# The second feed-forward product of a decoder layer as seven half-size block products instead of eight

## The reference

```
h += sqrelu(RMSNorm(h) @ W1) @ W2          # W1 1024 x 4096, W2 4096 x 1024
h += sigmoid(RMSNorm(h) @ W_gate) * (p @ W_ple)
return rmsnorm(h, final_norm_g)
```

## Time and profile before

| | us |
|---|---|
| median of 3 runs (lowest, highest) | 771.75 (771.71, 771.85) |
| the profiled execution, its own time | 771.78 |
| its span, first to last instruction | 770.1 |
| TensorE busy | 757.4 |
| DVE busy | 436.1 |
| ACT busy | 326.3 |
| POOL busy | 87.4 |

### The profile page before, as it was taken

How to read it: one execution, slowest core, us unless ns; L and a number is a source line. 1 busy time by engine, 2 the same in 40 slices (tenths; PEclk the granted TensorE clock), 3 DMA queues, 4 the chain that set the end, 5 groups by cost and what they waited for, 6 DMA issues and landing times.

```text
span 770.1 us, 9090 instructions
## 1 busy us (share of the span) xinstructions
PE 757.4 (98%) x3492; PEld 623.7 (81%) x3492; DVE 436.1 (57%) x488; ACT 326.3 (42%) x456; POOL 87.4 (11%) x60
## 2 busy tenths in 40 slices
PE   8999999999999999999999999999999999999996
PEld 7888877887887888888888888888888888888885
DVE  5556894668569575547454443444444444446754
ACT  6525447645475812326443140413223140323556
POOL 1022210864562000000000000000000000000000
PEclk9999999999999999999999999999999999999999
DMA  9622323432422443123423232332323232332102
GB/s 334 191 83 83 109 79 119 133 109 87 161 82 83 144 157 136 42 69 108 127 93 110 82 110 96 95 107 84 109 82 109 82 100 96 102 120 82 47 0 110
DMA packets 35193, 81.88 MB, mean 106 GB/s; under 512 B 3924, under 2 KB 5592, under 8 KB 35160
## 3 DMA queue, kind: packets, MB, share of 16 engines
q1 hardware_dynamic: 33928, 77.20, 30.8%
q10 hardware_dynamic: 1232, 4.23, 1.7%
HBM read 79.28 MB, written 2.13 MB: 106 GB/s over the span
## 4 chain that ended last, share of the span: by engine, by line
PE 93%; DVE 3%; ACT 1%; issue 1%; DMA 1%; SPq 0%; ACTq 0%; DVEq 0%
PE acc L1122 29%; PE acc L1124 29%; PE acc L1123 29%; PE side L1184 3%; PE side L1277 2%; DVE w_lo L751 1%; PE side L1244 1%; DVE conv L948 1%; DMA gain<-in_norm_mix_g 1%; PE side L1284 1%; PE side L1272 1%; DVE h L937 0%; PE acc L1201 0%; ACT w_hi L431 0%; PE side L1224 0%
## 5 line engine op out<-in xcount | busy, mean ns | idle before, releaser
L1122 PE MATMUL acc<-w_hi,a_hi 128*128 128x512 f32 x512 | 204.2, 399 | 0.0
L1124 PE MATMUL acc<-w_hi,a_lo 128*128 128x512 f32 x512 | 199.7, 390 | 0.0
L1123 PE MATMUL acc<-w_lo,a_hi 128*128 128x512 f32 x512 | 199.3, 389 | 0.0
L431 ACT ACTIVATE w_hi<-w_raw 128x1024 fp32r<-128x1024 f32 (+1 forms) x128 | 130.2, 1036 | 145.5 <-PE acc L1124 143.3
L751 DVE TENSOR_TENSOR w_lo<-w_raw,w_hi 128x1024 fp32r<-128x1024 f32 (+1 forms) x128 | 166.1, 1298 | 45.0 <-ACT w_hi L431 44.3
L802 DVE TENSOR_TENSOR h<-h,acc 128x1024 f32<-128x1024 f32 x48 | 58.6, 1220 | 106.1 <-PE acc L1124 106.0
L1122 PEld LDWEIGHTS acc<-w_hi,a_hi 128*128 128x128 f32 x512 | 96.2, 188 | 21.0 <-issue 1.4
L1123 PEld LDWEIGHTS acc<-w_lo,a_hi 128*128 128x128 f32 x512 | 96.2, 188 | 20.7 <-issue 1.4
L1124 PEld LDWEIGHTS acc<-w_hi,a_lo 128*128 128x128 f32 x512 | 96.1, 188 | 20.4
L1122 PE MATMUL acc<-b_hi,w_hi 128*128 128x512 f32 x256 | 99.6, 389 | 0.0
L1123 PE MATMUL acc<-b_lo,w_hi 128*128 128x512 f32 x256 | 99.6, 389 | 0.0
(11 more groups left out here) (183 smaller groups left out, 818.7 us busy)
## 6 DMA issues: line engine op xcount, KB each, us to landing
w_raw<-in_w_ff SPq DMA_DIRECT2D x64, 512.0 KB, 3.5
w_raw<-in_w_in SPq DMA_DIRECT2D x36, 512.0 KB, 3.8
w_raw<-in_w_out SPq DMA_DIRECT2D x16, 512.0 KB, 3.4
h<-in_x SPq DMA_DIRECT2D x8, 512.0 KB, 4.3
seg<-cs_dram ACTq DMA_DIRECT2D x8, 512.0 KB, 3.8
w_raw<-in_w_ple_gate SPq DMA_DIRECT2D x8, 512.0 KB, 3.8
out<-y SPq DMA_DIRECT2D x4, 512.0 KB, 2.6
w_raw<-in_w_ple_proj SPq DMA_DIRECT2D x4, 256.0 KB, 2.6
```

Of the source, the lines that this page charges most:

```text
L431: act.activation(w_hi[:, half, 2 * p:2 * p + n, :], w_raw[:, p, 0:n, :], ACT.Copy).then_inc(hi_ready, 1)
L1122: pe.matmul(dst, st[0], mv[0], start=start, stop=False)
L1123: pe.matmul(dst, st[0], mv[1], start=False, stop=False)
L1124: return pe.matmul(dst, st[1], mv[0], start=False, stop=stop)
```

## The change

The hidden units are taken in four units of 1024 instead of eight pairs of 512. For each unit the second product is [A11 A12; A21 A22] times [B11 B12; B21 B22]: A is the unit's squares, positions halved (256) and hidden units halved (512); B is 1024 x 1024 of W2 in four quarters of 512 x 512. It is made in Winograd's form of seven products of 256 x 512 x 512 instead of eight, each of 24 matmuls:

- The sums of the activations S3 = A21 - A11, S1 = A21 - A22, S2 = A11 - S1, S4 = A12 - S2 are made by DVE; each, and A11 and both halves of A2, is split by ACT and DVE.
- The sums of the weights T3 = B12 + B22, T2 = B11 + T3, T1 = B12 + B11, T4 = T2 + B21 are made by transfers that GpSimd issues with an add (`t_add`), in two halves of 512 KB each, into the buffer of one operand. T1 needs B12 again, which SP reloads when T2 has landed (`reload_b12`).
- The order is B11, T3, T2, T1, T4, B21, B22. B11 and T1 accumulate in two banks of `side` each over all four units, the others go to `acc` and are added to quarters of `h` by DVE in each unit (`h_add`, six additions of 128 x 1024). `h` holds combinations of its quarters until six more operations of the last unit (`h_finish`), two of which read no PSUM.

The first product of a unit is made of four forms of 512 x 512 (two column blocks, each in two halves of k), 48 matmuls each. Forms stand in a ring of three (`ring`, hi beside raw, lo in the place of raw), 11 per unit; a form may be loaded, or a quarter's hi written, only when the product of the form three before has ended. DVE no longer squares; ACT does (`square`). All loops are written out. The stage's buffers lie where `w_raw`, `w_hi`, `w_lo`, `a_hi`, `a_lo` and `y` were; so the first W1 forms are loaded only when the output projection has ended (before, the first block was split beside the per-layer product), and the per-layer product is stored to DRAM and loaded again ahead of the gate. The first group of the stage uses bank 2 of `acc`, not bank 0. The norm ahead of the gate takes row tiles 2, 3, 0, 1 (`TILES`): 2 and 3 are final after T4, 0 and 1 after B22; the first tile is transposed in the middle of B22, the second in the middle of the first gate group, the others after the second. The gate takes both column halves of tiles 2 and 3 first, and its first group waits for the B22 addition.

The diff, cut (of the last lists DVE's order is the first, TensorE's the last):

```diff
+TILES = (2, 3, 0, 1)
...
+PRODUCTS = ("B11", "T3", "T2", "T1", "T4", "B21", "B22")
+A_FORMS = ("A11", "S3", "S2", "S1", "A22", "A12", "S4")
+QUARTER = {"T3": 0, "T1": 0, "B12": 0, "B11": 1, "T2": 1, "T4": 1, "B21": 2, "B22": 3}
...
+            def load_f1(n):
+                u, e = divmod(n, FORMS)
+                b, kh = 2 * u + e // 2, e % 2
+                if n >= 3:
+                    sp.wait_ge(ff_step, form_end(n - 3))
+                else:
+                    sp.wait_ge(acc_full, 4 * (OUT + 4) if n < 2 else 4 * (PLE + 1))
...
+            load_f1(2)
+            load_quarter(0, "B22")
+            load_quarter(0, "B21")
+            load_f1(3)
+            reload_b12(0)
+            for u in range(1, UNITS):
+                load_quarter(u, "B12")
+                load_quarter(u, "B11")
+                load_quarter(u, "B21")
+                load_f1(FORMS * u)
+                load_quarter(u, "B22")
+                for e in range(1, 4):
+                    load_f1(FORMS * u + e)
+                reload_b12(u)
...
+            def t_add(u, name, p):
+                at = (slice(None), slice(2 * p, 2 * p + 2))
+                k = 8 * u + 2 * p
+                if name == "T3":
+                    pool.wait_ge(q_landed[0][p], 16 * (2 * u + 1))
+                    pool.wait_ge(q_landed[3][p], 16 * (u + 1))
+                    src = quarter[3][at]
+                elif name == "T2":
+                    sum_landed(pool, u, "T3", p)
+                    pool.wait_ge(form_lo, form_count(u, "B11", p))
+                    src = quarter[0][at]
+                elif name == "T1":
+                    pool.wait_ge(q_landed[0][p], 16 * (2 * u + 2))
+                    src = w_ff2[:, k:k + 2, 0:512]
+                else:
+                    pool.wait_ge(form_lo, form_count(u, "T2", p))
+                    pool.wait_ge(q_landed[2][p], 16 * (u + 1))
+                    src = quarter[2][at]
+                pool.dma_start(quarter[QUARTER[name]][at], src, accum_op=ALU.add
+                               ).then_inc(t_landed[QUARTER[name]][p], 16)
...
+                if j < 4:
+                    act.wait_ge(f1_landed[n % 3][p], 16 * f1_use(n))
+                    src = raw[at]
+                else:
+                    name = PRODUCTS[j - 4]
+                    src = quarter[QUARTER[name]][at]
+                    if name in SUMS:
+                        sum_landed(act, u, name, p)
+                    else:
+                        act.wait_ge(q_landed[QUARTER[name]][p], 16 * (u + 1))
+                    act.wait_ge(ff_step, form_end(n - 3))
+                act.activation(hi[at], src, ACT.Copy).then_inc(form_hi, 1)
...
+                bank, hq, op = {
+                    "T3 right": (acc[:, 0:2, :], h22, ALU.add), "T3 above": (acc[:, 0:2, :], h12, ALU.subtract),
+                    "T2": (acc[:, 2:4, :], h22, ALU.add), "T4": (acc[:, 0:2, :], h21, ALU.add),
+                    "B21": (acc[:, 2:4, :], h11, ALU.add), "B22": (acc[:, 0:2, :], h12, ALU.add)}[what]
...
+                src, hq, op = {
+                    "B11 above": (side[:, 0:2, :], h11, ALU.add), "B11 right": (side[:, 0:2, :], h22, ALU.subtract),
+                    "T1 right": (side[:, 2:4, :], h22, ALU.add), "T1 left": (side[:, 2:4, :], h21, ALU.add),
+                    "C21": (h22, h21, ALU.subtract), "C12": (h22, h12, ALU.add)}[what]
...
+            for u in range(UNITS):
+                n = FORMS * u
+                if u:
+                    for p in range(2):
+                        split_form(n + 1, p)
+                    h_add(u - 1, "B22")
...
+                for p in range(2):
+                    split_form(n + 6, p)
+                split_a(u, "S2")
+                split_a(u, "S1")
+                split_a(u, "A2a")
+                split_a(u, "A2b")
+                for p in range(2):
+                    split_form(n + 7, p)
+                h_add(u, "T3 right")
+                h_add(u, "T3 above")
+                split_a(u, "S4")
+                if u == UNITS - 1:
+                    h_finish("B11 above")
+                    h_finish("B11 right")
+                for p in range(2):
+                    split_form(n + 8, p)
+                h_add(u, "T2")
+                for p in range(2):
+                    split_form(n + 9, p)
+                if u == UNITS - 1:
+                    h_finish("T1 right")
+                    h_finish("T1 left")
+                    h_finish("C21")
+                for p in range(2):
+                    split_form(n + 10, p)
...
+                    h_finish("C12")
+                h_add(u, "T4")
+                if u < UNITS - 1:
+                    h_add(u, "B21")
+                    for p in range(2):
+                        split_form(n + FORMS, p)
+            for p in range(2):
+                split_lo(GATE, p)
+            normed(2, 0)
+            normed(2, 1)
+            for p in range(2, 4):
...
+                    left, c0 = s_form[int(name[1])][0::2], 0
+                else:
+                    left, c0 = a2[0::2], 256 if name == "A22" else 0
+                bank = {"B11": side[:, 0:2], "T1": side[:, 2:4], "T3": acc[:, 0:2], "T2": acc[:, 2:4],
...
+                if i >= 4:
+                    pe.wait_ge(gate_act, i - 3)
+                else:
+                    pe.wait_ge(h_added, add_count(UNITS - 1, "B22" if i < 2 else "B21"))
...
+            gate(0, lambda: turn_norm(2, 1))
+            gate(1)
+            turn_norm(2, 2)
```

More of the change, by code:

```diff
@@ L177, in build_layer @@
         kind = {}
-        for b in range(GATE + 2):
+        for b in range(PLE + 1):
             if b in (OUT, OUT + 1, OUT + 2, OUT + 3):
@@ L259, in freed, with form_end, f1_use, product_end @@
             ins.then_inc(side_free[fills[name][0]], 1)
+        def form_end(n):
+            u, j = divmod(n, FORMS)
+            return STEPS * u + (4 * j + 4 if j < 4 else 16 + 2 * (j - 4) + 2)
+        def f1_use(n):
+            return sum(m % 3 == n % 3 and m % FORMS < 4 for m in range(n + 1))
+        def product_end(u, name):
+            return STEPS * u + 16 + 2 * PRODUCTS.index(name) + 2
+        def form_count(u, name, p):
+            return 2 * (FORMS * u + 4 + PRODUCTS.index(name)) + p + 1
+        def sum_landed(eng, u, name, p):
+            eng.wait_ge(t_landed[QUARTER[name]][p], 16 * (2 * u + (1 if name in ("T3", "T2") else 2)))
+        ADDS = ("T3 right", "T3 above", "T2", "T4", "B21", "B22")
+        LAST_ADDS = ("B11 above", "B11 right", "T1 right", "T1 left", "C21", "C12")
+        def add_count(u, what):
+            return 2 + len(ADDS) * u + ADDS.index(what) + 1
+        LO_COUNT = {"A11": 1, "S3": 2, "S2": 3, "S1": 4, "A22": 6, "A12": 6, "S4": 7}
         block = ctx.enter_context(nc.Block())
@@ new lines, in relu, with square @@
+            def relu(u, i):
+                n = 8 * u + i
+                act.wait_ge(ff_step, STEPS * u + (5 + i if i < 4 else 9 + i))
+                if n >= 2:
+                    act.wait_ge(hid_raw, n - 1)
+                else:
+                    wait_filled(act, ("xt", 1, 2 + i, 1))
+                act.activation(tmp[:, i % 2, :], acc[:, (i + 2) % 4, :], ACT.Relu).then_inc(relu_done, 1)
+            def square(u, i):
+                n = 8 * u + i
+                act.wait_ge(relu_done, n + 1)
+                if i == 0 and u:
+                    act.wait_ge(s_raw, 7 * u)
+                if i == 4 and u:
+                    act.wait_ge(ff_step, product_end(u - 1, "B21"))
+                dst = a1[:, i, :] if i < 4 else a2[1][:, i - 4, :]
+                act.activation(dst, tmp[:, i % 2, :], ACT.Square).then_inc(hid_raw, 1)
@@ L760, in normed @@
                 slot, use = ((0, 1), (0, 3), (1, 3))[n]
+                c = s if n < 2 else TILES[s]
                 if s == 0:
```

580 lines of the change are left out of this document (394 added, 186 removed).

## The result

The changed kernel takes 758.38 us (median of four runs, 758.33 to 760.71) against 771.75: a ratio of 0.9827, 95% interval 0.9815 to 0.984. The prediction was 757.4 us, faster. The profiled execution took 760.71 us (span 759.0, mean granted clock 0.991); the other three had a span of 756.6 us at 0.995.

What follows compares the result with a forecast made beforehand. TensorE, busy 757.4 of 770.1 us, was taken as the bound, so fewer matmuls pay in full. 771.8 - 21.8 + 1.2 (turns) + 1.1 (stage start) + 5.1 (stage end) = 757.4 us; range 754 to 770.

Steps and rivals of the forecast that it cites:

- The 96 matmuls, -21.8 us: Feed-forward second product: 672 matmuls instead of 768, each 0.2267 us, all of it on the path.
- No stall inside the second half of a unit: From B11 on in each unit, DVE's queue has each form 3 to 6 us ahead of its product.
- Rival (d): DVE takes 1.22 instead of 1.14 us each; last B22 late, turns lose cover: 762; 0.19 together with the clock rival.
- The adding transfers: Weight sums, eight of 512 KB per unit: occupancy 3.2 us, landing 5.1 us after 1 us on GpSimd, no stall.
- that sign: Sign of being right: T4's half sums land by 13 us after B11 in the units.
- The limit: Chain T2, reload of B12, T1, T4: 2L + 3s under 29.4, so occupancy s up to 5.1 us with L = s + 1.9.
- the rival: Slow sums make T4 and T1 late in each unit; gain spent at s = 5.8, 782 to 788 at 6.3; chance 0.13.
- Rival (b), sums held by DVE: GpSimd writes descriptors only while DVE pauses; T4 sums 7 us late per unit, 28 in all, 785; chance 0.06.
- The turns of the units, +1.2 us: Next unit's third group waits for B22's addition: 1.3 us of cover, 0.4 us lost at each of three turns.
- The start of the stage, +1.1 us: First group goes to bank 2, so TensorE waits for ACT's copy of the last per-layer product.
- The end of the stage, +5.1 us: Last unit, waits on DVE's queue: 0.2 us before B22, 1.0 in its middle, 3.9 before the first gate product.
- The clock, rival (c), 2.6 us: Wait before the gate drops the clock to 1.2 GHz, some 3 us more: 760.5; 0.19 together with slower DVE.

Runs made afterwards that it cites:

- e1: Changed kernel with the 24 matmuls of T3 done twice in each unit, so 96 matmuls are back: 780.36 us.
- e3: Changed kernel with one plain 512 KB copy issued by GpSimd ahead of each of the 32 adding transfers: 763.79 us.
- e4: Changed kernel with two plain 512 KB copies issued by GpSimd ahead of each of the 32 adding transfers: 808.5 us.
- e9: Changed kernel run again without an edit, beside the kernel before on one chip: ratio 0.9824; profiled execution 756.83 us.
- e6: Changed kernel with unit 0's first product beginning in bank 0 instead of bank 2: 758.69 us.
- e11: Changed kernel with e6's bank order, e7's edits, T4's addition ahead of C12, and B22's addition ahead of the next second form's splits at turns: 752.11 us.
- e7: Changed kernel with gate products beginning in banks 2 and 3, and DVE doing B21's addition and first tile's lo parts before two gate-weight splits: 755.30 us.
- e12: e11 with the first normalised tile ahead of the two splits of gate weights on DVE: 752.67 us.

## Why the prediction was right, step by step

**The 96 matmuls, -21.8 us.** Right: 21.6 in e1, 3396 instructions, and units 81.6 to 81.7 us apart.

**No stall inside the second half of a unit.** Right, and the ledger of DVE's queue holds. In unit 0 B11 starts at 413.9 us; the form T4 was put at 18.4 us behind it, and DVE ends it 18.9 behind, as the timeline of the kernel after shows. Rival (d), DVE at 1.22 instead of 1.14 us each, did not come: behind the split at 429.32 the next starts 1.13 us later. Only the two additions to h take 1.23 us each (two from 426.86 to 429.32).
```profile
426.86 2.54 DVE L1331 TENSOR_TENSOR h<-h,acc 128x1024 f32<-128x1024 f32 x2
429.32 1.22 DVE L1314 TENSOR_TENSOR s_lo<-s_raw,s_hi 128x1024 fp32r<-128x1024 f32 x1
430.45 2.35 DVE L1275 TENSOR_TENSOR ring_lo<-quarter,ring_hi 128x1024 fp32r<-128x1024 f32 x2
```

**The adding transfers.** Occupancy was taken as 3.2 us and measured at 2.9. The Trainium skill, "Collectives: The Full Stack", section on the bandwidth ceiling, has an adding transfer at half the rate of a copy; here it is 2.9 to 1.57, a factor of 1.86. Landing was put at 5.1 us after 1 us on GpSimd; the page has 6.1 from the issue. For T4 the landing was forecast by 13 us behind B11, and ACT took the second half up at 14.0, released by the transfer: 1 us later than that sign allowed, with 7 us of cover left to the 21 at which the prediction has it needed. The limit was mis-sized: it set L = s + 1.9, as for a transfer that has the engines for itself. In e3 the adding transfers landed after 10.5 us at s = 4.4, with a copy and loads on the same engines. The give-back starts below s = 4.4 and not at 5.1, and by the line it is half again as steep (30 and not 20 us for each us); the fallen clock of e4 is in that. By the estimate above the gain is spent at 4.7, not at the 5.8 of the prediction: the rival was nearer than told, though with the measured 2.9 us still well clear.

**Rival (b), sums held by DVE.** Empty. GpSimd's two issues of T4's sums in unit 0, and ACT's use of the second, in the timelines of the kernel after:
```profile
419.30 0.88 POOL L570 DMA_DIRECT2D quarter<-quarter  x1 [5.80 <-DVE ring_lo L1275]
420.43 0.85 POOL L570 DMA_DIRECT2D quarter<-quarter  x1 [0.25 <-DVE ring_lo L1275]
...
427.90 1.06 ACT L659 ACTIVATE ring_hi<-quarter 128x1024 fp32r<-128x1024 f32 x1 [1.75 <-DMA quarter<-quarter]
```
DVE is busy without a pause from 417.8 to 436 us, and the second sum has landed 7.5 us after its issue. The Trainium skill, "SBUF — State Buffer", section "Who interferes with whom", says that a sum of two tensors on DVE does not stall such a transfer; the trace agrees.

**The turns of the units, +1.2 us.** The cover was computed as 1.3 us; slower loads and sharing were then taken to use it up and 0.4 us more, a loss of 1.7. In the kernel after, B22's addition ends at 457.03 and the third group wants it at 457.47:
```profile
453.41 2.48 DVE L1275 TENSOR_TENSOR ring_lo<-ring_raw,ring_hi 128x1024 fp32r<-128x1024 f32 x2 [3.12 <-ACT ring_hi L659]
455.81 1.22 DVE L1331 TENSOR_TENSOR h<-h,acc 128x1024 f32<-128x1024 f32 x1
```
0.44 us of cover are left: the loss of cover was 0.9 and not 1.7, so there was no wait. In e9, the same kernel, the addition ends 2.0 us ahead at this turn, and in e6 and e3 there were waits of 0.36 and 0.42 us: the cover changes with the execution. The term should have been 0 to 0.4, not 1.2. With the order of e11, addition first, it ends 5.4 us ahead (451.92 for 457.30).

**The start of the stage, +1.1 us.** Right: 1.31 by the profile, 1.5 from start to start, with the releaser as named, and gone in e6.

**The end of the stage, +5.1 us.** Right in kind. By the profile's waits it is 4.4 us: 0.49, 0.62 and 3.28 us for 0.2, 1.0 and 3.9. The prediction reckoned from start to start; so counted it is 4.9 (0.65, 0.8 and 3.4), 0.2 less than forecast. The order of what waits for what was as computed. DVE's queue is unbroken from 671.5 to 702.7 us in the kernel after.

**The clock, rival (c), 2.6 us.** It was given as a case of its own with 3 us. It came in the profiled execution and, in six others with the same wait, in one more; the median does not hold it (758.38 against 760.71). It fits a term with a chance, not a case.

**What was missing.** The start of the kernel, early or late by 1.4 us, was not in the range of causes: the profile of before was of an early one. From start to start, the turns (-1.2), the end (-0.2) and the start of the stage (+0.4) came out 1.0 us better than forecast; the slower instructions behind the waits, some 0.5 us, had no term, and the late start cost 1.4: 757.4 - 1.0 + 0.5 + 1.4 = 758.3 against 758.38. The mechanism was right; that the number came within 1.0 us is in part luck, as a term of 1.2 us for waits that did not come made up for most of a loss that nobody had seen. Without the late start the kernel took 756.83.

## What to carry to other kernels

Where TensorE has no gap, matmuls taken out pay in full. What has to be worked out is the queue of the helpers in the shortest stretch, and the places where a stage begins and ends. Here the banks decided: let the first product of the next stage take the bank that comes free first (e6, and e7 with its order on DVE: 4.4 us here). Reordering a queue that has no pause moved the wait (e11, e12). Less work in it, or moving what is not needed ahead of the wait behind it, should shorten it; e7 did the second, together with its change of banks, and taking work out was not tried. A transfer that lay well hidden cost nothing until its cover ended, and then stalls, and with two copies the clock too: test the distance by slowing it, not by making it smaller.

## What the runs showed of the hardware

- An adding transfer of 512 KB from SBUF to SBUF holds the 16 engines for 2.9 us and lands 6.1 us after its issue; one of 64 KB in pieces of 256 bytes still holds them for 0.8 us.
- GpSimd's instruction for it takes 0.87 us (mean of 24), and its end says nothing of the data, which lands some 5 us later. The Trainium skill, "Perfetto Trace Analysis", section "DMA Instruction — SWDGE (GPSIMD)", says the same of this instruction.
- The same code, with the same wait of 3.28 us on TensorE, is followed by a granted clock of 0.50 for some 7 us in one execution (after) and by 1.00 in another (e9). The 20 short matmuls at the start of the kernel ran at either level too, and 1.4 us remain between the two.
- The clock can fall behind shorter waits: in e4 behind waits of 2.1 and 2.7 us, while in e3 it stayed at 1.00 behind one of 2.76.
